# Flat activation tiles, and the climb of addresses moved into the weights' slots of some groups

## What is computed

```python
# first block
h    = rmsnorm(x, norm_pre_w)                     # (256, 2048)
proj = h @ w_in                                   # q k v o z | gates i f | u zb | ga gb
qk   = silu(causal_conv(concat(q, k)))
ht   = mlstm(q, k, v, log_i, log_f)               # 8 heads
y_a  = sigmoid(o) * norm(ht) * silu(z)
y_b  = (pool(u) @ pool_w) * pool_scale * silu(zb)
merged = sigmoid(ga) * (y_a @ w_proj_mlstm) + sigmoid(gb) * (y_b @ w_proj_pool)
x    = x + rmsnorm(merged @ w_out)
# second block: two attentions (differential, latent) on h = [meta; x]
h    = h + concat(oA * silu(a_g), oB * silu(b_g)) @ w_out_2
out  = rmsnorm(h)[16:272]
```

## Time and profile before

| | |
|---|---|
| median of 3 runs | 1461.4 us (1460.16 to 1461.64) |
| the profiled execution's own time | 1462.16 us |
| its span | 1460.5 us |
| TensorE matmul busy | 1435.6 us, 98% |
| VectorE, ScalarE busy | 850.6 us (58%), 707.5 us (48%) |
| mean granted TensorE clock | 0.995 |
| DMA | 266 MB, mean 182 GB/s |

### The profile page before, as it was taken

One profiled execution on the slowest core, in us unless ns is written; L12 is line 12 of the kernel. 1 busy time (PEld: TensorE's weight loads), 2 busy tenths in 40 slices (PEclk: granted clock), 3 DMA queues, 4 the chain that ended last, 5 costly groups with the idle time before them and its releaser, 6 DMA issues.

```text
span 1460.5 us, 27819 instructions
## 1 busy us (share of the span) xinstructions
PE 1435.6 (98%) x10878; PEld 1370.6 (94%) x10878; DVE 850.6 (58%) x1054; ACT 707.5 (48%) x929; POOL 63.1 (4%) x95
## 2 busy tenths in 40 slices
PE   6999999999999999999999999999999999999997
PEld 6999998899999999999999999888999999999786
DVE  5676674546655666545454545556555545667754
ACT  5545544545555444434344444446433346667543
POOL 0000000001110000000000000001000002111000
PEclk8999999999999999999999999999999999999999
DMA  6655645655555555555655556656555553334553
GB/s 228 201 190 184 201 166 192 196 178 177 168 175 193 175 186 190 174 194 182 199 189 191 193 190 214 247 173 217 203 172 169 178 174 121 121 121 136 208 198 122
DMA packets 71940, 266.01 MB, mean 182 GB/s; under 512 B 8088, under 2 KB 8096, under 8 KB 70944
## 3 DMA queue, kind: packets, MB, share of 16 engines
q1 hardware_dynamic: 69840, 253.12, 51.9%
q0 software_dynamic: 1440, 10.63, 2.1%
q10 hardware_dynamic: 576, 1.05, 0.2%
HBM read 260.56 MB, written 4.20 MB: 181 GB/s over the span
## 4 chain that ended last, share of the span: by engine, by line
PE 93%; DVE 3%; ACT 1%; DVEq 1%; issue 1%; DMA 0%; ACTq 0%; POOL 0%; SPq 0%; POOLq 0%
PE ps L350 23%; PE ps L354 22%; PE ps L352 22%; PE ps L342 6%; PE ps L343 6%; PE ps L344 6%; PE ps L462 2%; DVE wl L1220 1%; DVEq L1215 1%; PE ps L748 1%; PE ps L540 1%; PE ps L551 1%; DMA xn<-in_x 0%; PE ps L589 0%; ACT wh L900 0%
## 5 line engine op out<-in xcount | busy, mean ns | idle before, releaser
L1220 DVE TENSOR_TENSOR wl<-raw,wh 128x1024 fp32r<-128x1024 f32 x474 | 580.0, 1227 | 501.1 <-ACT wh L900 492.6
L900 ACT ACTIVATE wh<-raw 128x1024 fp32r<-128x1024 f32 x474 | 499.9, 1060 | 555.9 <-PE ps L354 426.7
L350 PE MATMUL ps<-xh,wh 128*128 128x256 f32 x1792 | 499.7, 279 | 3.0 <-DVE xl L1229 1.8
L352 PE MATMUL ps<-xl,wh 128*128 128x256 f32 x1792 | 498.0, 278 | 0.0
L354 PE MATMUL ps<-xh,wl 128*128 128x256 f32 x1792 | 497.9, 278 | 0.0
L350 PEld LDWEIGHTS ps<-xh,wh 128*128 128x128 f32 x1792 | 337.9, 189 | 3.7 <-DVE xl L1229 2.2
L352 PEld LDWEIGHTS ps<-xl,wh 128*128 128x128 f32 x1792 | 338.1, 189 | 0.1
L354 PEld LDWEIGHTS ps<-xh,wl 128*128 128x128 f32 x1792 | 338.0, 189 | 0.0
L350 PE MATMUL ps<-x2h,wh 128*128 128x256 f32 (+1 forms) x688 | 199.2, 290 | 1.0 <-DVE avt L1387 0.4
L354 PE MATMUL ps<-x2h,wl 128*128 128x256 f32 (+1 forms) x688 | 194.8, 283 | 0.0
L352 PE MATMUL ps<-x2l,wh 128*128 128x256 f32 (+1 forms) x688 | 194.5, 283 | 0.0
(11 more groups left out here) (337 smaller groups left out, 1772.8 us busy)
## 6 DMA issues: line engine op xcount, KB each, us to landing
raw<-in_w_stream SPq DMA_DIRECT2D x474, 512.0 KB, 3.3
xn<-in_x SPq DMA_DIRECT2D x4, 512.0 KB, 7.7
xr<-in_x POOLq DMA_DIRECT2D x1, 2048.0 KB, 12.3
x_kept<-xr POOLq DMA_DIRECT2D x1, 2048.0 KB, 9.1
x1r<-x_kept POOLq DMA_DIRECT2D x1, 2048.0 KB, 10.0
mrow<-bound_rows POOLq DMA_DIRECT2D x8, 128.0 KB, 3.5
poolw<-in_pool_w POOLq DMA_DIRECT2D x1, 1024.0 KB, 6.3
postw<-in_post_w POOLq DMA_DIRECT2D x1, 1024.0 KB, 5.2
```

The lines of the kernel that those rows point to most:

```text
L350: pe.matmul(out_at(j), whr[:, c, f], hi(kc)[:, tokens], start=st, stop=False, skip_group_check=True)
L352: pe.matmul(out_at(j), whr[:, c, f], lo(kc)[:, tokens], start=False, stop=False, skip_group_check=True)
L900: act.activation(slot_view(wh_at[r], layout), raw[r][:, :, :], ACT.Copy).then_inc(wh_done, 1)
L1220: tt(slot_view(wl_at[r], layout), raw[r][:, :, :], slot_view(wh_at[r], layout).bitcast(F32), ALU.subtract).then_inc(split_done, 1)
```

## The change

The tiles x, y and z lose their ramp: chunk kc begins at kc x 256. Their weights begin at 48 in the slot, (48, 512), in ordinary groups. In the groups of `CLIMBS_AT` and in all OZ groups, two slots, from the named slot on, have (60, 516) and (52, 516), with the two chunks of the slot taken in reverse order; in the first group the slots ahead of these stand at (64, 512). V's weights go from (16, 512) to (0, 512). R_Z and R_V move down by 80 and 32 elements, to multiples of 64, and xl, yl, zl lie 64 elements closer to xh, yh, zh. The first three slots of V and WO now take the layout of a turn in the loop of the stage before.

```diff
-RAMP = [4 * min(kc, 4) for kc in range(KC + 1)]
-ON_RAMP, TOKEN_RAMP = (0, 512), (16, 512)
-LAYOUT_OF = {"qk": ON_RAMP, "o": ON_RAMP, ..., "pb": ON_RAMP, "v": TOKEN_RAMP, "wo": BY_TOKEN, ...
+FLAT, CLIMB = (64, 512), ((60, 516), (52, 516))
+LAYOUT_OF = {"v": BY_TOKEN, "wo": BY_TOKEN, "uv": BY_TOKEN, "w2": BY_TOKEN, ...
+CLIMBS_AT = {("QK", 0, 0): 3, ("UZ", 0, 0): 0, ("UZ", 0, 1): 0, ("UZ", 1, 0): 0, ("MG", 0, 0): 0}

 def slot_layouts():
+    def layout(name, i, j, kind, k):
+        at = 0 if name == "OZ" else CLIMBS_AT.get((name, i, j))
+        if at is not None and k < at + len(CLIMB):
+            return CLIMB[k - at] if k >= at else FLAT
+        return LAYOUT_OF.get(kind, BY_FEATURE)          # BY_FEATURE = (48, 512)
...
         if name in ("V", "WO"):
-            of[:LEAD] = last[:LEAD]
+            of[:LEAD] = looped
+        per = len(of) // times
+        looped = of[per:per + LEAD]

-    R_X, R_C, R_Y, R_Z, R_V, R_T = 51200, 86016, 118784, 151872, 168576, 185024
+    R_X, R_C, R_Y, R_Z, R_V, R_T = 51200, 86016, 118784, 151552, 168448, 185024

     def slot_view(slot, layout):
         first, pitch = layout
-        return slot[:, first:first + SLOT_KC * pitch].rearrange("p (c n) -> p c n", n=pitch)[:, :, 0:COLS]
+        skip = max(0, first + SLOT_KC * pitch - SLOT_W)
+        return slot[:, first - skip:first - skip + SLOT_KC * pitch].rearrange(
+            "p (c n) -> p c n", n=pitch)[:, :, skip:skip + COLS]

-    xh = sb("xh", [P, KC * S + RAMP[KC]], F32R, R_X)
-    xl = sb("xl", [P, KC * S + RAMP[KC]], F32R, R_X + 16640)
+    xh = sb("xh", [P, KC * S], F32R, R_X)
+    xl = sb("xl", [P, KC * S], F32R, R_X + 16384)
...
-        return lambda kc: t[:, kc * S + RAMP[kc]:(kc + 1) * S + RAMP[kc]]
+        return lambda kc: t[:, kc * S:(kc + 1) * S]
...
-            for c, j in [(c, j) for j in js for c in range(SLOT_KC)] if by_columns else [
-                    (c, j) for c in range(SLOT_KC) for j in js]:
+            cs = range(SLOT_KC)[::-1] if layout in CLIMB else range(SLOT_KC)
+            for c, j in [(c, j) for j in js for c in cs] if by_columns else [(c, j) for c in cs for j in js]:
                 kc = k * SLOT_KC + c
-                a, z = kc == 0, kc == kcs - 1
+                a, z = k == 0 and c == cs[0], kc == kcs - 1
```

More of the change, by code:

```diff
@@ L70 @@
 SLOT_W = 1088
-RAMP = [4 * min(kc, 4) for kc in range(KC + 1)]
 BY_FEATURE, BY_TOKEN, SECOND, SECOND_KEYS = (48, 512), (0, 512), (0, 528), (16, 528)
-ON_RAMP, TOKEN_RAMP = (0, 512), (16, 512)
-LAYOUT_OF = {"qk": ON_RAMP, "o": ON_RAMP, "z": ON_RAMP, "u": ON_RAMP, "zb": ON_RAMP, "ga": ON_RAMP, "gb": ON_RAMP, "pa": ON_RAMP, "pb": ON_RAMP,
-             "v": TOKEN_RAMP, "wo": BY_TOKEN, "uv": BY_TOKEN, "w2": BY_TOKEN, "cq": SECOND_KEYS, "ckv": SECOND_KEYS,
+FLAT, CLIMB = (64, 512), ((60, 516), (52, 516))
+LAYOUT_OF = {"v": BY_TOKEN, "wo": BY_TOKEN, "uv": BY_TOKEN, "w2": BY_TOKEN, "cq": SECOND_KEYS, "ckv": SECOND_KEYS,
              "ak": SECOND_KEYS, "av": SECOND_KEYS, "aq": SECOND, "g": SECOND}
+CLIMBS_AT = {("QK", 0, 0): 3, ("UZ", 0, 0): 0, ("UZ", 0, 1): 0, ("UZ", 1, 0): 0, ("MG", 0, 0): 0}
 def slot_layouts():
-    out, last = [], []
+    def layout(name, i, j, kind, k):
[3 more added lines that the diff above has]
+        return LAYOUT_OF.get(kind, BY_FEATURE)
+    out, looped = [], []
     for name, kinds, times in STAGES:
-        of = [LAYOUT_OF.get(kind, BY_FEATURE) for kind in kinds for _ in range(slots_of(kind))] * times
+        of = [layout(name, i, j, kind, k) for i in range(times) for j, kind in enumerate(kinds)
+              for k in range(slots_of(kind))]
         if name in ("V", "WO"):
-            of[:LEAD] = last[:LEAD]
+            of[:LEAD] = looped
+        per = len(of) // times
+        looped = of[per:per + LEAD]
         out += of
-        last = of
     return out
@@ L144, in slot_view, with chunked @@
         first, pitch = layout
-        return slot[:, first:first + SLOT_KC * pitch].rearrange("p (c n) -> p c n", n=pitch)[:, :, 0:COLS]
-    xh = sb("xh", [P, KC * S + RAMP[KC]], F32R, R_X)
-    xl = sb("xl", [P, KC * S + RAMP[KC]], F32R, R_X + 16640)
-    def ramped(t):
-        return lambda kc: t[:, kc * S + RAMP[kc]:(kc + 1) * S + RAMP[kc]]
+        skip = max(0, first + SLOT_KC * pitch - SLOT_W)
[3 more added lines that the diff above has]
+    xl = sb("xl", [P, KC * S], F32R, R_X + 16384)
+    def chunked(t):
+        return lambda kc: t[:, kc * S:(kc + 1) * S]
     def four(t, i):
-        first, pitch = (0, S + RAMP[1]) if isinstance(i, int) and i == 0 else (i * 4 * S + RAMP[4], S)
-        return t[:, bass.ds(first, 4 * pitch)].rearrange("p (c n) -> p c n", n=pitch)[:, :, 0:S]
+        return t[:, bass.ds(i * 4 * S, 4 * S)].rearrange("p (c n) -> p c n", n=S)
     def plain(t):
@@ L162, in build_program @@
     qk = sb("qk", [P, 2 * KC, S], F32, R_C)
-    yh = sb("yh", [P, KC * S + RAMP[KC]], F32R, R_Y)
-    yl = sb("yl", [P, KC * S + RAMP[KC]], F32R, R_Y + 16640)
+    yh = sb("yh", [P, KC * S], F32R, R_Y)
+    yl = sb("yl", [P, KC * S], F32R, R_Y + 16384)
     xn = sb("xn", [P, TOK, D], F32, R_Y)
     xsq = sb("xsq", [P, TOK, D], F32, R_C)
-    zh = sb("zh", [P, KC // 2 * S + RAMP[KC]], F32R, R_Z)
-    zl = sb("zl", [P, KC // 2 * S + RAMP[KC]], F32R, R_Z + 8448)
+    zh = sb("zh", [P, KC // 2 * S], F32R, R_Z)
+    zl = sb("zl", [P, KC // 2 * S], F32R, R_Z + 8192)
     vn = sb("vn", [P, TOK, H * VW], F32, R_V)
@@ L323, in free @@
             def free(c, at):
-                if k == 0 and c == 0:
+                if k == 0 and c == cs[0]:
                     for s, v, o in frees:
@@ L500, in groups @@
                 off += slots_of(kind)
-        X, Y, Z = (ramped(xh), ramped(xl)), (ramped(yh), ramped(yl)), (ramped(zh), ramped(zl))
+        X, Y, Z = (chunked(xh), chunked(xl)), (chunked(yh), chunked(yl)), (chunked(zh), chunked(zl))
         def x_there(j, kind, k):
@@ L518, in _ @@
             o = ps[0:GATE_W, 4, 0:S]
-            pe.matmul(o, wgh[:, kc, :], ramped(xh)(kc), start=kc == 0, stop=False)
-            pe.matmul(o, wgl[:, kc, :], ramped(xh)(kc), start=False, stop=False)
-            last = pe.matmul(o, wgh[:, kc, :], ramped(xl)(kc), start=False, stop=kc == KC - 1)
+            pe.matmul(o, wgh[:, kc, :], chunked(xh)(kc), start=kc == 0, stop=False)
+            pe.matmul(o, wgl[:, kc, :], chunked(xh)(kc), start=False, stop=False)
+            last = pe.matmul(o, wgh[:, kc, :], chunked(xl)(kc), start=False, stop=kc == KC - 1)
         last.then_inc(s_gate_sums, 1)
@@ L921, in _ @@
             act.wait_ge(s_x_turned, b + 1)
-            high_parts(ramped(xh), b, "norm_pre", s_x_high)
+            high_parts(chunked(xh), b, "norm_pre", s_x_high)
             if b + 1 < LEAD:
@@ L1244, in x_low_parts @@
         def x_low_parts(b):
-            low_parts(ramped(xl), ramped(xh), b, "norm_pre", s_x_high, s_x_low)
+            low_parts(chunked(xl), chunked(xh), b, "norm_pre", s_x_high, s_x_low)
         x_rstd(0)
```

## The result

The changed kernel takes 1478.86 us (median of 4, 1478.2 to 1480.08) against 1461.14 us before (median of 4): a ratio of 1.0123, 95% interval 1.0106 to 1.0141. It is 1.2% slower, where 0.5% faster was forecast. Rival A, the fast spacing is never reached, had been priced at 1478.8 us.

What follows compares the result with a forecast made beforehand. TensorE, busy 98%, was taken to bound the kernel through its matmul spacing. Gains of 4.7+1.6+0.2+0.3-0.2+1.0+0.1 = 7.7 us off the median 1461.4 gave 1453.7 us, range 1451.9 to 1457.0.

Steps and rivals of the forecast that it cites:

- Rival A: Fast matmul spacing never reached by moving weights down under still tiles, or lost at a boundary; about 1478.8 us; chance 0.06.
- Term 1: 19 ordinary groups without a climb (QK, UZ 1/1, MG) go from 22.01 to 21.76 us each, 4.7 us gained.
- Term 2: The four pb groups go from 11.27 to 10.88 us each, 1.6 us gained.
- Term 3: First group: climb in slots 3 and 4, so chunks 10 to 15 run at 113.3 ns; 0.2 us gained.
- Rival B: Only the first group's climb fails, leaving the seven QK groups behind it at 117.8 ns; 1460.0 us; chance 0.11.
- Terms 4 to 6: Weight and buffer places in V, WO, W2 and uv: V gains 0.3 us, WO loses 0.2, W2 gains 1.0, uv 0.1.
- Term 7: UQ goes from 16 to -16 without a climb, taken at nothing, at most 0.6 us gained; gates and heads near nothing.
- Term 8: Other engines: ACT's rounding and DVE, working behind TensorE, are not slowed by the new slot offsets; no cost.
- C: Relative place is no cause and a group's head is slow as such; no change, 1461.4 us; chance 0.05.

Runs made afterwards that it cites:

- e2_abs: Kernel before, with x tiles and their groups' weight slots moved up together by 48 elements, the tile still climbing; 1460.7 us.
- e9_mirror: e5_hold with the extra matmuls' weights stepping down ahead of QK 0/1 and their tile falling ahead of MG 0/0; 1491.1 us.
- e5_hold: Changed kernel plus 48 extra matmuls with a rising tile ahead of QK 0/1 and of MG 0/0, whose slot climb is removed; 1474.2 us.
- e11_kept: Kernel before, x ramp kept, y and z flat 16 elements up, V's weights climbing with x, oh, oall, ol and gates moved; 1457.25 us, ratio 0.9978.
- e10_spiral: Kernel before, x ramp of 4 per chunk over all 16 chunks, weights following, y and z flat; 1485.4 us.
- e3_follow: Kernel before with its tile ramp, weights climbing along in groups that follow no burst, so the relative place stays -16; 1473.4 us, ratio 1.0083.

## Why the prediction was wrong

**The step that failed** is the sentence behind "The change part by part": "That is the same ladder in the same number of matmuls, so those twelve cost what they do now." It took the relative place for the whole cause of the rhythm. The ladder by the weights ends at 117.8 ns, at the relative and absolute places (e2_abs, e9_mirror against e5_hold) where the ladder by the tile ends at 113.3. So 31 groups take 0.6 us more than before, where 12 were to stay and 19 to gain 0.25.

Point by point:

Term 1, the 19 groups: forecast 21.76 us each, measured 22.61. The argument that a flat group holds the spacing was right: e5_hold shows 21.76 for QK from its second group on, and 21.76 and 10.88 in MG. It only had nothing to hold. The prediction had said that a stretch at 117.8 would mean that it had misjudged how the fast spacing is held; what it misjudged is how it is reached. The lower bound of the term, -0.6 us a group, was the value.

Term 2, pb: forecast 10.88, measured 11.30, for the same reason; 10.88 in e5_hold and e11_kept.

Term 3, the first group: its last 72 matmuls took 43.96-35.48 = 8.48 us, as before. The climb behind the wait failed like all others. Rival B had only this one fail; since the weights' climb fails everywhere, its cause (x still being written, the wait) is not needed, and no run tests it by itself.

Terms 4 to 6: V 0.1 us a group gained, WO +0.23, W2 0.32 a group, each within 0.02 us of the working. In these the relative place was enough to tell the spacing, since nothing steps there once the first slots are past.

Term 7: UQ at (1217.95-1200.99)/144 = 117.8 ns, as taken. It moved from 16 to -16 and stayed slow. Missed there: the two uk groups, which moved alike, went from 123.4 to 126.5 ns a matmul, 0.14 us lost, and uv gained 0.17. The gate matmuls and the heads between the groups moved by 0.02 us at most.

Term 8: ACT and DVE as busy as before, TensorE's wait ahead of W2's chunk 12 is 1.48 us in place of 1.42. Nothing was hidden or given back there.

The rivals: A was right, in its price (1478.8 us against 1478.9) and in its ground ("isn't reached by moving the weights down under tiles that stand still"). I gave it 0.06. What I held against it, the unmarked boundary from gb to pb, bears only on its second half, losing the spacing; nothing in the trace of before spoke against its first half, since no weights ever stepped under a flat tile there. An effect whose history matters had been seen in one way only, and I carried it to another way by a symmetry that no row showed. C is refuted: flat heads cost what the rest of the group costs, in both rhythms. By the traces, matmuls of one shape come every 113.3 or 117.8 ns by nothing but the operands' addresses and their order. The rule of the Trainium skill on which the prediction built its rival of no change ("SBUF — State Buffer", section "SBUF: two separate sides") is that no other user of SBUF makes PE wait. No run here tests that; that addresses cost nothing doesn't follow from it, and the spacings show that they do cost.

Two sums of the prediction are off, and nothing hangs on them. Terms 4 to 6 add up to 1.2 us and not to the 1.3 that A's price takes off. The lower end of the range, 1451.9 us, isn't what the two gains give that it names: 1453.7 less 0.6 and 0.2 is 1452.9.

What stays open is why TensorE tells the two ways apart. The relative places in a climb by the tile and in one by the weights are the same number by number, so something besides that difference must enter: perhaps where each operand stands against its own predecessor. That is a guess, suggested by e10_spiral, e3_follow and e9_mirror, and not shown.

## What to carry to other kernels

Where a dense stream of matmuls has two rhythms at the same addresses, treat the rhythm as a state: look for what enters it, what leaves it, and what merely keeps it, and test each by one group ahead of moving a whole layout. Once in the good state, keep both operands where they stand modulo 64 elements; in these runs even a step of both together by the same 4 elements lost it. And when a chance is given to "this equivalent form has the same effect", ask which row shows the equivalence; here a climb by the weights ahead of a single group would have shown it.

## What the runs showed of the hardware that was not expected

At full clock a 128x128 by 128x256 fp32r matmul comes every 113.3 or 117.8 ns at one and the same pair of places; which one depends on the way there. With the moving tile stepping up by 4 elements, 12 matmuls at each place, from 0 to -16, it is 113.3. With steps of 8, with 1, 3 or 6 matmuls at a place, and with weights falling from 0 (12 or 24 matmuls at a place), it is 117.8; so it is with a tile falling or weights rising from -32. The fast spacing lasted 304 us through the waits at group starts, loop edges and changes of PSUM bank, and was lost within a chunk when both operands stepped by 4 together. The 128x512 form costs 226.7 ns at a relative place of 0 and 233 at -16 (230.0 in W2, whose high part lay at 32 and low part at 16), and needs no climb: behind the first three slots of V it fell to 226.7 by itself. At a relative place of 0 that both operands keep by joint steps of 4 it costs 229 to 232 (e11_kept).
